# An expert layer's activations turned by ScalarE and VectorE instead of TensorE, with the down weights loaded in four parts

## What is computed

```python
def expert_block(args):                      # MOE_BLOCK = 128 rows of one expert
    tok, e = args
    xb = xt[tok]
    gate = jnp.minimum(xb @ w_gate[e] + b_gate[e], SWIGLU_LIMIT)
    up = jnp.clip(xb @ w_up[e] + b_up[e], -SWIGLU_LIMIT, SWIGLU_LIMIT)
    act = (up + 1.0) * gate * jax.nn.sigmoid(SWIGLU_ALPHA * gate)
    return act @ w_down[e] + b_down[e]
```

## Time and profile before

| what | value |
|---|---|
| median of 3 runs | 2354.96 us (2352.86 to 2360.63) |
| profiled execution, first to last instruction | 2352.5 us |
| PE busy | 2191.9 us (93%) |
| DVE, ACT, POOL busy | 1021.4, 466.7, 444.8 us |
| HBM read | 480.51 MB |
| loop over the jobs | about 720 to 2305 us |

### The profile page before, as it was taken

The page is one execution under the profiler, slowest core; times in us unless marked ns, Lnnn a source line. Parts: engine busy times, 40 slices in busy tenths (PEclk is TensorE's granted clock), DMA queues, the critical chain, the costliest instruction groups (busy, mean ns, idle before and its releaser), DMA issues.

```text
span 2352.5 us, 33568 instructions
## 1 busy us (share of the span) xinstructions
PE 2191.9 (93%) x9959; PEld 1018.7 (43%) x9960; DVE 1021.4 (43%) x1587; ACT 466.7 (20%) x624; POOL 444.8 (19%) x417
## 2 busy tenths in 40 slices
PE   5889999879968999999999899999999999999995
PEld 3444444464544444443443344444443444444442
DVE  3575754465775243444334243423253333222235
ACT  2334434331220111111111111111111111111113
POOL 0010100001231122222222132312213222122110
PEclk9989999889968999999999999999999999999997
DMA  8222221012252776889489999747899558897644
GB/s 330 84 67 69 89 72 36 1 73 84 89 214 91 240 296 213 298 291 400 135 284 399 355 354 407 256 158 246 297 376 349 204 174 297 291 324 240 214 128 154
DMA packets 168969, 510.55 MB, mean 217 GB/s; under 512 B 16434, under 2 KB 51002, under 8 KB 167770
## 3 DMA queue, kind: packets, MB, share of 16 engines
q1 hardware_dynamic: 153802, 474.25, 53.9%
q0 software_dynamic: 15120, 35.67, 6.9%
HBM read 480.51 MB, written 31.46 MB: 218 GB/s over the span
## 4 chain that ended last, share of the span: by engine, by line
PE 85%; DVE 7%; DMA 3%; issue 2%; ACT 1%; SPq 1%; DVEq 0%; POOL 0%; POOLq 0%
PE psall L605 27%; PE psall L633 14%; PE psall L609 10%; PE psall L776 10%; PE psall L637 5%; PE psall L614 4%; PE psall L764 3%; PE psall L887 2%; PE psall L881 2%; DMA arena<-in_w_down_dram 2%; PE psall L674 1%; PE psall L743 1%; DMA arena<-in_x_dram 1%; PE psall L642 1%; DVE arena L1423 1%
## 5 line engine op out<-in xcount | busy, mean ns | idle before, releaser
L605 PE MATMUL psall<-arena 128*128 128x512 f32 x1472 | 645.7, 597 | 27.5 <-issue 22.3
L605 PEld LDWEIGHTS psall<-arena 128*128 128x128 f32 x1472 | 278.6, 191 | 373.0 <-issue 373.0
L633 PE MATMUL psall<-arena 128*128 128x512 f32 x736 | 323.5, 598 | 4.8 <-DVE arena L1792 3.2
L609 PE MATMUL psall<-arena 128*64 128x512 f32 x1152 | 258.5, 600 | 8.9 <-DVE arena L1629 3.7
L1618 DVE STREAM_TRANSPOSE arena<-arena 128x1024 f32<-128x1024 f32 x49 | 61.0, 1246 | 453.6 <-PE psall L605 276.5
L776 PE MATMUL psall<-arena 128*128 128x512 f32 (+1 forms) x608 | 246.5, 563 | 0.7 <-ACT arena L1037 0.7
L633 PEld LDWEIGHTS psall<-arena 128*128 128x128 f32 x736 | 139.5, 191 | 183.3 <-issue 183.3
L1217 ACT COPY arena<-psall 128x512 f32<-128x512 f32 x49 | 28.7, 586 | 792.1 <-PE psall L674 792.1
L1792 DVE COPY arena<-psall 128x512 f32<-128x512 f32 x49 | 33.9, 692 | 323.3 <-PE psall L674 323.1
L776 PEld LDWEIGHTS psall<-arena 128*128 128x128 f32 x608 | 116.5, 192 | 120.6 <-issue 116.3
L1220 ACT ACTIVATE arena<-arena 128x1024 f32<-128x1024 f32 x49 | 51.8, 1057 | 582.5 <-DVE arena L1626 582.5
(11 more groups left out here) (319 smaller groups left out, 2098.6 us busy)
## 6 DMA issues: line engine op xcount, KB each, us to landing
arena<-in_w_gate_dram SPq DMA_DIRECT2D x128, 1024.0 KB, 6.5
arena<-in_w_up_dram SPq DMA_DIRECT2D x128, 1024.0 KB, 8.6
arena<-in_w_down_dram SPq DMA_DIRECT2D x128, 1024.0 KB, 8.9
arena<-in_w_ada_dram SPq DMA_DIRECT2D x16, 1024.0 KB, 5.3
arena<-in_w_ada_dram SPq DMA_DIRECT2D x4, 2048.0 KB, 14.2
arena<-in_w_in_dram SPq DMA_DIRECT2D x16, 512.0 KB, 4.0
arena<-in_x_dram SPq DMA_DIRECT2D x2, 2048.0 KB, 28.4
arena<-in_w_out_dram SPq DMA_DIRECT2D x1, 4096.0 KB, 14.1
```

Of the source, the lines that this page charges most:

```text
L605: mm = pe.matmul(ps[2 * g + s], xT[:, k, :], w[:, s * BANK:(s + 1) * BANK], start=(k == 0), stop=(k == KD - 1))
L609: mm = pe.matmul(ps[2 * g][HT * j:HT * j + HT, :], xT[:, k, 0:HT], w[:, j * BANK:(j + 1) * BANK], start=(k == 0), stop=(k == KD - 1), skip ...
L633: mm = pe.matmul(ps[6 + s], aT[:, k, :], w[:, s * BANK:(s + 1) * BANK], start=(k == 0), stop=(k == KD - 1))
```

## The change

TensorE no longer turns the activations. Instead `act_rows` (a new 128x1024 tile) takes them in a layout in which one VectorE block transposition gives `aT`:

- kind 4: 16 ScalarE copies of 32 partitions by 256 elements, each from a quarter of `ub` to another group of 32 partitions of `act_rows`; kinds 3 and 2: 8 such copies; kind 1: none, since `swiglu` writes the quarter part straight to `act_rows` (the last product of `swiglu` is one instruction for each of the two parts in kind 3, one before).
- Then VectorE turns 4, 3, 2 or 1 groups of 256 columns in 32x32 blocks in one instruction (`turn_act`), which stands where its copy from PSUM stood. It waits for `act_spread`, and `down` waits for `aT_ready` alone.
- Block turning gives another order of the contraction: row (a, k, i) of the weight, a of 4, k of 8, i of 32, meets partition 32a+i. So each 1 MB down piece comes in four loads, each of 32 partitions by 2 rows of 4 KB, and the semaphore counts 64 for a piece.

```diff
             def dn_pieces(e, u):
                 for q in range(DNP):
                     sp.wait_ge(dn_used, DNP * u + (q + 1))
-                    w_v = w_down[0].rearrange("e (q c p) n -> e q p c n", c=2, p=P)[:, q]
-                    sp.dma_start(ring[GUP + q], w_v[ds(e, 1)].rearrange("a p c n -> p (a c) n")).then_inc(d_dn[q], 16)
+                    w_v = w_down[0].rearrange("e (a k i) n -> e a i k n", a=4, k=KD)
+                    for a in range(4):
+                        sp.dma_start(ring[GUP + q][QR * a:QR * a + QR],
+                                     w_v[ds(e, 1), a, :, 2 * q:2 * q + 2].rearrange("x i c n -> i (x c) n")).then_inc(d_dn[q], 16)
...
         def down(pe, kind, u, order_):
-            pe.wait_ge(aT_act, u + 1)
-            pe.wait_ge(aT_dve, u + 1)
+            pe.wait_ge(aT_ready, u + 1)
             pe.wait_ge(y_biased, u + 1)
+            landed = pe.snap(order_ * 4, min_val=64, max_val=64 * NE)
...
-                            by_kind(pe, t, lambda kind: gate_up(pe, kind, u, on_, 0, KD // 2))
+                            by_kind(pe, t, lambda kind: gate_up(pe, kind, u, on_, 0, KD))
                             tp, op_ = typ_of(pe, typ_p), ord_of(pe, ord_p, wait_p)
-                            with pe.If(tp > 0):
-                                pe.wait_ge(act_ready, u + 1)
-                                by_kind(pe, tp, lambda kind: turn(pe, ub, JOB_KINDS[kind][2] // P, JOB_KINDS[kind][1] // P).then_inc(act_turned, 1))
-                                pe.nop()
-                            by_kind(pe, t, lambda kind: gate_up(pe, kind, u, on_, KD // 2, KD))
...
+            def spread(u, kind):
+                act.wait_ge(act_ready, u + 1)
+                if kind == 1:
+                    act.nop().then_inc(act_spread, 1)
+                    return
+                if kind == 4:
+                    moves = [(t, a, QW * a) for t in range(4) for a in range(4)]
+                else:
+                    moves = [(t, 2 * j + h, QW * h) for t in range(2) for j in range(2) for h in range(2)]
+                for t, a, c in moves:
+                    of = QR * t + (0 if kind == 4 else HT * (a // 2))
+                    mm = act.copy(act_rows[QR * a:QR * a + QR, QW * t:QW * t + QW], ub[of:of + QR, c:c + QW])
+                mm.then_inc(act_spread, 1)
...
-                            act.wait_ge(act_turned, u + 1)
-                            act.copy(aT[:, 0:4].rearrange("p k n -> p (k n)"), ps[4]).then_inc(aT_act, 1)
+                            by_kind(act, typ_of(act, typ_p), lambda kind: spread(u, kind))
+                            act.nop()
...
+            def turn_act(kind):
+                lo, hi = JOB_KINDS[kind][1] // QW, JOB_KINDS[kind][2] // QW
+                dve.transpose(aT.rearrange("p b (t s) -> p t b s", t=4)[:, lo:hi],
+                              act_rows.rearrange("p (t b i) -> p t b i", t=4, b=KD)[:, lo:hi]).then_inc(aT_ready, 1)
...
-                            dve.wait_ge(act_turned, u + 1)
-                            dve.tensor_copy(aT[:, 4:8].rearrange("p k n -> p (k n)"), ps[5]).then_inc(aT_dve, 1)
+                            dve.wait_ge(act_spread, u)
+                            settle(dve)
+                            by_kind(dve, tp, turn_act)
```

More of the change, by code:

```diff
@@ L240, in layer @@
         aT = reg(o, KD, P); o += 1024
+        act_rows = reg(O_X1 + 19456, D)
         yb = reg(o, D); o += 1024
@@ L312, in layer @@
             sem("g_biased"), sem("sg_ready"), sem("u_clipped"), sem("ug_ready"), sem("act_ready"))
-        act_turned, aT_act, aT_dve = sem("act_turned"), sem("aT_act"), sem("aT_dve")
+        act_spread, aT_ready = sem("act_spread"), sem("aT_ready")
         y_dve, y_stored, yq_stored, yb_free = sem("y_dve"), sem("y_stored"), sem("yq_stored"), sem("yb_free")
@@ L626, in down @@
                     if k % 2 == 0 and sweep == sweeps[0]:
-                        pe.wait_ge(d_dn[k // 2], order_)
+                        pe.wait_ge(d_dn[k // 2], landed)
                         if kind < 4:
@@ L641, in down @@
                         for j in range(4):
-                            mm = pe.matmul(ps[7][QR * j:QR * j + QR, 0:QW], aT[:, 4 + k % 2, QR * (k // 2):QR * (k // 2) + QR],
+                            mm = pe.matmul(ps[7][QR * j:QR * j + QR, 0:QW], aT[:, k, HT:HT + QR],
                                            w[:, j * QW:(j + 1) * QW],
@@ L670, in ord_of @@
             return eng.snap(bounded, min_val=16, max_val=16 * NE)
-        def turn(pe, src, n, first=0):
-            for k in range(first, n):
-                mm = pe.transpose(psT[:, k * P:(k + 1) * P], src[:, k * P:(k + 1) * P], ident[:, :])
-            return mm
         @block.tensor
@@ L974, in job_lists @@
                 mm.then_inc(half_mm, 1)
-            pe.nop().then_inc(act_turned, 1)
             pe.wait_ge(tab_ready, 16)
@@ L1640, in swiglu @@
                 dve.wait_ge(ug_ready, u + 1)
-                dve.scalar_tensor_tensor(out=ub[:, w], in0=sg[:, w], scalar=s7, in1=ub[:, w], op0=ALU.min,
-                                         op1=ALU.mult).then_inc(act_ready, 1)
+                for p0, p1, c, b, n in parts:
+                    if p0 == 0:
+                        w = slice(c, c + n)
+                        mm = dve.scalar_tensor_tensor(out=(act_rows if c else ub)[:, w], in0=sg[:, w], scalar=s7, in1=ub[:, w],
+                                                      op0=ALU.min, op1=ALU.mult)
+                mm.then_inc(act_ready, 1)
+            def turn_act(kind):
+                lo, hi = JOB_KINDS[kind][1] // QW, JOB_KINDS[kind][2] // QW
+                dve.transpose(aT.rearrange("p b (t s) -> p t b s", t=4)[:, lo:hi],
+                              act_rows.rearrange("p (t b i) -> p t b i", t=4, b=KD)[:, lo:hi]).then_inc(aT_ready, 1)
             first_ranks(NT - 1, NT + 1)
@@ L1705, in _ @@
             turn_rows_in()
-            dve.nop().then_inc(aT_dve, 1)
+            dve.nop().then_inc(aT_ready, 1)
             dve.nop().then_inc(act_ready, 1)
```

4 lines of the change are left out of this document (1 added, 3 removed).

## The result

| | before | after |
|---|---|---|
| median | 2354.57 us (2352.86 to 2360.63) | 2489.81 us (2483.77 to 2498.43) |
| profiled execution, span | 2352.5 us | 2482.1 us |
| granted clock of TensorE, mean of the span | 0.967 | 0.945 |
| ratio of the times, 95% interval | | 1.057 (1.0549 to 1.0590) |

The changed kernel is 5.7% slower, 135 us. The direction was forecast, the size was not: 2424 us stands 66 us too low, the range ends 3 us too low, and rival B gave 2484.

The account below looks back on a forecast made before the run. TensorE was taken to bound the expert loop, with DMA nearly late. Terms -23 + 8 + 67 + 10 + 7 = +69 us on the 2352.5 us span gave 2421.5, a median of 2424 us; range 2338 to 2487 us.

Parts of the forecast that it names:

- rival B: Down loads: a full halving of their rate, 5.3 us a piece, +129 us, 2484 us; chance 0.20.
- What bounds the kernel: Expert loop: TensorE sets the pace, busy 1364.5 of 1400 us; DMA nearly late, mean share 0.77.
- What leaves TensorE, -23 us: Expert loop: 288 transposes of 0.12 us, 35 us, gained in 9 of 14 stretches: -23 us.
- What ScalarE and VectorE take on, +8 us: Chain from last product to down: copies 0.40 us, turning 1.25 us, 7.7 us in all; late at few jobs, +8 us.
- crowded: Five 100 us stretches of the expert loop with DMA share 0.91 to 1.00, where the engines idle only 24 us.
- The price of a piece, 4.4 us: Down loads into 32 partitions: 2.63 us divided by a rate ratio of 0.60, 1.75 us more a piece.
- The reach of it, 67 + 10 us: Dearer down pieces on the path: +67 us for 52 pieces in crowded stretches, +10 us for the other 76.
- The clock, +7 us: TensorE after long waits: slower work, as a half gate_up took 9.96 us instead of 7.09; 0 to 30, taken +7 us.
- A: Down loads keep their rate, so the kernel gets faster: 2333 us; chance 0.17.
- C: Down loads lose mildly, 3.1 to 3.8 us a piece: +13 us, about 2368 us; chance 0.13.
- D: Turning chain decides: loads keep their rate, copies take 0.6 us or more, chain 11 us: 2353 us; chance 0.03.
- What would show it: Signs: down waits 60 to 90 us, gate/up 20 to 50, 300 to 340 GB/s; 1500 to 1600 us unchanged but for turning.

Follow-up runs that it names:

- the doubled turning: The kernel before, with every transposition on TensorE done twice: 2382.35 us, ratio 1.0114.
- the spaced loads: The kernel before, with each down piece in four loads of 32 partitions lying four apart: 2365.24 us, ratio 1.0028.
- two halves: The kernel before, with each down piece in two loads of 64 neighbouring partitions: 2492.87 us, ratio 1.0563.
- four parts in alternation: The changed kernel, with the four parts of a piece issued in the order 0, 2, 1, 3: 2464.18 us, ratio 1.0474.
- the split alone: The kernel before, turning still on TensorE, with each down piece in four loads of 32 neighbouring partitions: 2492.05 us, ratio 1.0567.
- wide twin: The changed kernel with one wide load per down piece in the old row order, so it computes another sum: 2349.89 us, ratio 0.9966.

## Why the forecast was right in sign and short in size

**What bounds the kernel: half right.** That TensorE sets the pace and DMA is nearly late was right. What was wrong was to read the slack from stretches of 100 us: nine experts of 30 to 36 us had a full DMA share from mark to mark while TensorE waited for none of their weights, and one of them, from 1804 to 1835 us, stands in no stretch called crowded; it alone lost 16 us.

**What leaves TensorE, -23 us: too much.** By the doubled turning 288 transposes are 28 us of path. In the trace with wide loads 16 us more went into waits for weights and some 6 into the chain; by the medians 8 us are left. With the split loads nothing that can be measured is left.

**What ScalarE and VectorE take on, +8 us: right.** 402 ns and 1245 ns, `down` of the last job 8.3 us behind its product (forecast 7.7), three small waits of 1.3 to 2.3 us at other full jobs. The slow last `down` adds nothing to it: 16.0 us here, 16.6 before.

**The price of a piece, 4.4 us: nearly right.** 4.7 us by engine time. By the stretch of narrow loads alone (225 GB/s at a share of 1.04) it is 4.7 us too. The ratio of 0.60 from one stretch should have been 2.63 / 4.7 = 0.56; a wide load ran beside the narrow ones in it, as the forecast had noted. SP's extra issues had been put at nothing; the spaced loads bound them and all else that the number of loads brings at 7 us.

The rule of the Trainium skill (SBUF — State Buffer, "Door 1: The DMA port swizzle") holds in every comparison made here: 32 neighbouring partitions and 64 neighbouring ones are equally slow (1.0567, 1.0563), as both reach half of the ports, and 32 that lie four apart reach all by its table and are as fast as 128 but for 7 us. By its 218 GB/s a piece takes 4.8 us, an estimate; the trace says 4.7. The same page says that two loads at partitions 0 and 64 together are only 6% faster than one (section "Can I just issue two DMAs to hit both halves?"). No run here loads one half alone, so the figure itself was not tested. That such loads don't repair each other is borne out: two halves took 4.7 us a piece, and with four parts in alternation engine time fell by 0.35 of 4.7 us.

**The reach of it, 67 + 10 us: the step that failed.** The forecast put 224 us of engine time on the DMA engines and 77 us on the path, a third. Measured: 259 us against the same kernel with wide loads, and 140 us of time (2489.8 - 2349.9), more than half. By the marks of SP the stretches called crowded lost 92 us, where the forecast had 67; with the measured price its own sum gives 52 x 2.06 - 24 = 83. The others lost 36 us net of what was saved there, where the forecast's terms come to -23 + 8 + 10 = -5. So the larger part of the miss, 41 us, lies outside the crowded stretches, in the term of 10 us and in the saving that the late weights ate. The idle time of the DMA engines there, 298 us, had been counted as room. Most of it lies in experts with full jobs and can't be lent: the ring holds one expert, a load can't start before its place is free, and the late down pieces of a short expert are waited for at the start of the long one behind it, before the idle time comes (share 0.66 from 1175 us on).

**The clock, +7 us: wrong as a term.** With the same instructions the split alone makes TensorE busy for 50 us more, and between the changed kernel and its wide twin it is 43 us (2208.1 against 2165.2), beside 84 us more of idle time. The forecast saw one long wait with a slow half `gate_up` behind it; what came were 55 waits of at most 4 us close together, with slow groups between them. But these 43 us do not all add to the loss. In the nine experts with a full DMA share before and after, the loads set the length, and a slower matmul there most likely fills time that would else be a wait: the dearer pieces account for 74 of their 86 us, the other 12 stay open. How much the clock costs by itself in the others was not separated. What is certain is that idle time showed only 84 of the 126 us by which the two spans differ; the forecast added waits (77 us, near the 84) and clock as if the one bore no relation to the other.

**The rivals.** A is out: the rate is not kept, and by the wide twin its 22 us would have been 8. B came near the time by luck: with a piece of 5.3 us, dearer than the 4.7 measured, and a smaller reach than the measured one; the two errors cancel. C is out with a piece of 4.7 us. D does not hold in this kernel, with copies of 0.40 us, but its mechanism is real: at 0.65 us a copy, waits of 5 to 8 us at full jobs before quarter jobs are there.

**What would show it.** Waits for down pieces 60 to 90 us: 69. Gate and up 20 to 50: 42. 300 to 340 GB/s at full share: 286 to 332. From issue to landing a down load takes 13.1 us (median), before 8.9. Three signs came out while the time was 66 us off. They did not belong to the sum: the waits forecast here, 80 to 140 us, are more than the 77 us that it had taken for them, and for the slow work between the waits it had 7 us. The fourth sign failed: from 1500 to 1600 us nothing but the turning was to change, but the expert that holds most of it, 86.6 us before, took 5 us longer, with 7.3 us of waits for down pieces at its start.

## What to carry to other kernels

A load to a contiguous group of 32 or 64 partitions occupied the DMA engines 1.8 times as long as the same bytes to all 128 (4.7 us against 2.63 for 1 MB), so a layout that needs such groups has to be paid for before its gain is counted; where a layout allows it, spread the partitions of each load. Read the slack of a ring not from stretches of equal length but unit by unit: here the DMA share of each expert's own time, not only its weights' bytes, since other transfers run beside them. And waits in a trace can understate such a loss: between repeated waits TensorE worked more slowly, here 43 and 50 us of longer work beside 84 and 88 us of added idle time. Not all of that longer work adds to the loss: where the loads set the length, it stands in place of waits.

## What the runs showed of the hardware that had not been expected

- A matmul whose moving operand is read with a stride of 8 elements (32 bytes) takes 0.92 us instead of 0.44 for 512 columns. VectorE's block transposition of 128x1024 takes 2038 ns instead of 1245 with that stride, ScalarE's copy of 32x256 653 instead of 402. A note in the section on Door 1 of the same page of the Trainium skill says that SBUF gives full rate only while consecutive reads stay in a line of 16 bytes, four such elements; the three rows agree in kind.
- Adding 288 transposes to TensorE costs their full 28 us; taking them away gives back 8. In the trace without them TensorE waits 16 us more for weights and some 6 more for the chain that replaces them.
- A full `down` takes 15.7 to 16.8 us behind waits for the turning of 2.3 to 20.4 us, and 14.0 behind those of at most 1.7 us. Near 2 us both stand: 15.70 behind 1.99 us and 14.00 behind 2.14 (both with the strided transposition).
